# Sparse attention lane of one Trainium2 kernel, reordered by pairs of heads, with a planned moment for each part of a step

## The chip, the cores and the metric

One core of one Trainium2 chip runs the whole program. The metric is the device time of one execution in microseconds (us); lower is better. The kernel before has a median of 3911.82 us over three runs (3907.46 to 3923.37).

## What is computed

Two transformer blocks of two layers each on a sequence of 512 tokens and 1024 features, in float32. The change touches only the second block, which runs its attention stage twice, once per layer. There, six heads of 64 features in two key groups take part in three gated attentions:

```python
        s_s = jnp.einsum('bqgrd,bgqnd->bgrqn', qb, k_sel).astype(f32) * scale
        p_s = masked_softmax(s_s, key_pos <= tq[:, None])
        o_s = jnp.einsum('bgrqn,bgqnd->bqgrd', p_s.astype(v_sel.dtype), v_sel)
...
        s_w = jnp.einsum('bqgrd,bngd->bgrqn', qb, kw).astype(f32) * scale
        p_w = masked_softmax(s_w, m_w)
        o_w = jnp.einsum('bgrqn,bngd->bqgrd', p_w.astype(vw.dtype), vw)
        gt = jax.nn.sigmoid(gb.astype(f32))[..., None]
        return (gt[:, :, 0] * o_c + gt[:, :, 1] * o_s + gt[:, :, 2] * o_w).astype(qb.dtype)
```

`o_c` (not shown) goes over compressed keys, `o_s` over selected blocks, `o_w` over a window; `gt` are gates. At 512 tokens the selection and the window hold every earlier token, so that the kernel computes both as dense causal attention: the same queries against two sets of keys and values. These two are the "sparse lane". Beside it in the same stage stand the products that make the queries, keys and values of four "stick-breaking" heads, those heads themselves, the compressed attention, and a norm of each head's output.

## The kernel before, in words

The stage is `attention_region`. Each of its lanes writes a program per engine as a Python generator; a `yield` gives a planned time, and `weave` merges the lanes of an engine by these times into one fixed order of instructions. The planned times only set that order. On the chip every engine works strictly through its own list and waits at semaphores.

The lanes of the stage, by planned time in us from its start:

- the items lane (L635), 4 to 73: six products in three passes each (L493 to L495) with weights that ScalarE (L479) and VectorE (L484) split before;
- the compress lane (L2603 to L2633) and the compressed lane (L2663 to L2738), up to 76;
- the stick lane, 75 to 157: for each of four heads the scores in four blocks (L2890), masked by VectorE (L2932), then ScalarE's Abs, Exp and Ln (L2961, L2964, L2967), VectorE's L2940, running sums on TensorE (L2908) with VectorE's L2944 after each, ScalarE's Exp (L2973), the product with the values (L2920), and VectorE's copy L2950;
- the norms lane, 159 to 208: for each of eight tiles a square on ScalarE (L2999), a sum on TensorE (L3015), Ln and Exp on ScalarE (L549, L551), and a scaling on VectorE (L3022);
- the sparse lane, 2 to 198.

The sparse lane has three tiles `t` of two heads, four query blocks `qb` of 128 tokens and two kinds `m` of keys, hence 24 combinations, each for the heads `u` = 0 and 1: 48 items `n`, which it takes one after the other. The number of keys is 128, 256, 384 or 512 (`(qb + 1) * P`). An item is a score on TensorE (L2770), mask and row maximum on VectorE (L2809), the exponential with its sum on ScalarE (L2845), reciprocal, gate and scaling on VectorE (L2826, L2828, L2830), `qb + 1` transposes on TensorE (L2785), a copy out by ScalarE (L2858), and `qb + 1` products with the values on TensorE (L2796). After sixteen items VectorE adds the tile to the result (L2815), for which the norms of these tiles wait.

Head `u` = 0 lies in partitions 0 to 63 and head `u` = 1 in 64 to 127, for the queries and keys of a score as for the output of a product with values. Each step of the lane emits three parts at one planned time: on TensorE the score of item n + 2, the transposes of item n - 1, the products of item n - 2. Steps are equally long whatever their width:

```python
    def share(n):
        return (AHEAD + n) / (len(items) + 2 + AHEAD)
...
        for n in range(len(items) + 2):
            if n + 2 < len(items):
                score(n + 2)
            if 1 <= n <= len(items):
                t, qb, m, u = items[n - 1]
                pe.wait_ge(scaled, n)
```

In the trace a float32 matmul shows as two matmul records. Scores alternate between two PSUM banks (`logits[:, u]`), and a score waits until VectorE has read its bank (`shifted`).

Of the kernel before, what the change touches and what calls it, by code (L numbers as in the profile page):

```python
# [2742 lines left out]
def sparse_lane(k, r, lane, nq, ks2, kw2, vs_rows, vw_rows, cmp_out, gates, mixT, tile_out):  # L2743
# [3 lines left out]
    items = [(t, qb, m, u) for t in range(T) for qb in range(TC) for m in range(2) for u in range(2)]  # L2747
    PER_TILE = 4 * TC
# [5 lines left out]
    AHEAD = 0.6  # L2754
# [4 lines left out]
    def share(n):  # L2759
        return (AHEAD + n) / (len(items) + 2 + AHEAD)  # L2760

    @lane.tensor
    def _(pe):
        def score(n):
            t, qb, m, u = items[n]
            at, g = head(t, u)
            keys = (ks2, kw2)[m][int(g != u)]
            if n >= 2:
                pe.wait_ge(shifted, n - 1)
            nc.tensor.matmul(logits[:, u, 0:(qb + 1) * P], nq[at, t, qb * P:(qb + 1) * P], keys[at, 0:(qb + 1) * P],  # L2770
                             start=True, stop=True).then_inc(logit_done, 1)

        score(0)
        score(1)
        yield share(0)
        for n in range(len(items) + 2):
            if n + 2 < len(items):
                score(n + 2)
            if 1 <= n <= len(items):
                t, qb, m, u = items[n - 1]  # L2780
                pe.wait_ge(scaled, n)
                if n >= 3:
                    pe.wait_ge(turn_out, n - 2)
                for b in range(qb + 1):
                    last = nc.tensor.transpose(turned[:, u, b * P:(b + 1) * P], probs[:, (n - 1) % DEEP, b * P:(b + 1) * P], k.at["ident"])  # L2785
                last.then_inc(turn_done, 1)
            if n >= 2:
                t, qb, m, u = items[n - 2]
                at, g = head(t, u)
                to = out_ps[at, qb * P:(qb + 1) * P]  # L2790
                rows = (vs_rows, vw_rows)[m]
                if t and qb == m == u == 0:
                    pe.wait_ge(tile_out, t)
                pe.wait_ge(turn_out, n - 1)
                for b in range(qb + 1):
                    last = nc.tensor.matmul(to, rows[:, b, g * HD:(g + 1) * HD], probs_t[:, (n - 2) % DEEP, b * P:(b + 1) * P],  # L2796
                                            start=(m == 0 and b == 0), stop=(m == 1 and b == qb))
                last.then_inc(pv_done, 1)
            yield share(n + 1)

    @lane.vector
    def _(dve):
        def shift(n):
            t, qb, m, u = items[n]
            keys = (qb + 1) * P
            dve.wait_ge(logit_done, n + 1)
            if n >= DEEP:
                dve.wait_ge(turn_done, n - DEEP + 1)
            nc.vector.tensor_tensor_reduce(probs[:, n % DEEP, 0:keys], logits[:, u, 0:keys], k.at["causal_row"][:, S - keys:S],  # L2809
                                           -1.0, 3e38, ALU.add, ALU.min, neg_max[:, n % DEEP:n % DEEP + 1]).then_inc(shifted, 1)  # L2810

        def leave(t):
            dve.wait_ge(cmp_out, t + 1)
            dve.wait_ge(pv_done, PER_TILE * (t + 1))
            nc.vector.tensor_tensor(mixT[:, GDN_T + t, :], mixT[:, GDN_T + t, :], out_ps[:, :], ALU.add).then_inc(tile_out, 1)  # L2815

        shift(0)
        shift(1)
        yield share(0)
        for n in range(len(items)):  # L2820
            t, qb, m, u = items[n]
            p = n % DEEP
            at = probs[:, p, 0:(qb + 1) * P]
# [1097 lines left out]
```

## Time and profile before

| | us |
|---|---|
| median of three runs | 3911.82 |
| the profiled execution | 3889.2 |
| its span, first to last instruction | 3887.3 |
| TensorE matmul busy in it | 3528.6 (91%) |
| VectorE busy | 1789.5 (46%) |
| ScalarE busy | 1310.9 (34%) |
| first stage, TensorE's first to VectorE's last instruction | 2093.6 to 2314.5 |
| second stage, likewise | 3117.3 to 3338.3 |

In the rows PE is TensorE's matmul, PEld its weight load, DVE VectorE, ACT ScalarE, POOL GpSimd. A row of the timeline has start, duration from the first start to the last end, engine, line, operation, output and inputs, shapes, the number of instructions merged (x4), and in brackets the idle time before it with what ended that. The stage stands in the span twice; the rows of the two agree in their parts, and those of the first are used.

### The profile page before, as it was taken

What the parts mean: (1) busy time and instruction counts of PE and PEld (TensorE: products, weight loads), DVE (VectorE), ACT (ScalarE), POOL (GpSimd) and SP (SyncE); (2) the same over time, 40 slices, a digit from 0 to 9 for tenths busy, and PEclk for the clock granted to TensorE, in tenths of its full rate; (3) what the DMA queues carried; (4) which work ended last, traced back from release to release, by engine and by line L of the source; (5) the groups of instructions that cost most, each with busy time, mean ns of one, the idle gap of its engine ahead of it and who ended that gap; (6) DMA issues with size and microseconds to landing.
All of it is one profiled execution on the core that took longest, in us unless ns stands there. A gap on an engine that the chain in (4) does not pass through costs nothing. (4 is left out here: it accounts for less than half of the span.)

```text
span 3887.3 us, 46528 instructions
## 1 busy us (share of the span) xinstructions
PE 3528.6 (91%) x19333; PEld 2722.2 (70%) x19333; DVE 1789.5 (46%) x2765; ACT 1310.9 (34%) x2030; POOL 420.8 (11%) x351
## 2 busy tenths in 40 slices
PE   5999897999998799998998979999988899799998
PEld 4777765888686568886675647788766665477885
DVE  4775466443333433333534444444444435345534
ACT  2332453222322432322322343333343234433423
POOL 0001000220001102100122000310002300012100
PEclk7989998999999899998998999999999989899999
DMA  6651215333221112221202012232131020222230
GB/s 229 206 163 39 79 30 195 130 120 109 76 87 33 65 65 95 103 93 56 74 7 56 1 49 71 92 98 110 44 96 39 2 56 1 92 68 96 98 108 22
DMA packets 230431, 316.17 MB, mean 81 GB/s; under 512 B 13117, under 2 KB 167590, under 8 KB 228942
## 3 DMA queue, kind: packets, MB, share of 16 engines
q1 hardware_dynamic: 230222, 313.20, 24.4%
q8 instruction: 154, 2.52, 0.3%
q14 instruction: 55, 0.45, 0.0%
HBM read 310.52 MB, written 6.85 MB: 82 GB/s over the span
## 5 line engine op out<-in xcount | busy, mean ns | idle before, releaser
L493 PE MATMUL out<-h_lo,w_hi 128*128 128x512 f32 x2608 | 1042.6, 400 | 44.1 <-DVE w_lo L484 39.9
L494 PE MATMUL out<-h_hi,w_hi 128*128 128x512 f32 x2608 | 1021.7, 392 | 0.0
L495 PE MATMUL out<-h_hi,w_lo 128*128 128x512 f32 x2608 | 1021.2, 392 | 0.0
L484 DVE TENSOR_TENSOR w_lo<-ring,w_hi 128x1024 fp32r<-128x1024 f32 (+2 forms) x461 | 565.8, 1233 | 984.8 <-ACT w_hi L479 979.8
L479 ACT ACTIVATE w_hi<-ring 128x1024 fp32r<-128x1024 f32 (+2 forms) x461 | 470.9, 1027 | 1159.2 <-PE out L495 1075.1
L493 PEld LDWEIGHTS out<-h_lo,w_hi 128*128 128x128 f32 x2608 | 493.7, 189 | 168.3 <-issue 50.6
L494 PEld LDWEIGHTS out<-h_hi,w_hi 128*128 128x128 f32 x2608 | 493.6, 189 | 112.1 <-issue 11.0
L495 PEld LDWEIGHTS out<-h_hi,w_lo 128*128 128x128 f32 x2608 | 493.4, 189 | 103.8
L493 PE MATMUL item_banks<-h_lo,w_hi 128*128 128x512 f32 (+1 forms) x632 | 288.3, 456 | 14.4 <-DVE w_lo L484 5.1
L494 PE MATMUL item_banks<-h_hi,w_hi 128*128 128x512 f32 (+1 forms) x632 | 254.3, 402 | 0.0
L495 PE MATMUL item_banks<-h_hi,w_lo 128*128 128x512 f32 (+1 forms) x632 | 253.8, 402 | 0.0
L493 PEld LDWEIGHTS item_banks<-h_lo,w_hi 128*128 128x128 f32 (+1 forms) x632 | 121.6, 192 | 55.5 <-issue 22.0
L493 PE MATMUL item_banks<-w_lo,h_hi 128*128 128x256 f32 (+1 forms) x320 | 103.8, 324 | 43.4 <-DVE w_lo L484 27.3
L495 PEld LDWEIGHTS item_banks<-h_hi,w_lo 128*128 128x128 f32 (+1 forms) x632 | 121.0, 191 | 30.9
L494 PEld LDWEIGHTS item_banks<-h_hi,w_hi 128*128 128x128 f32 (+1 forms) x632 | 121.8, 193 | 28.3 <-issue 8.2
L1497 POOL TENSOR_TENSOR tiles<-temp 128x512 f32<-128x512 f32 x44 | 72.8, 1654 | 605.1 <-DVE temp L1483 324.9
L428 DVE SCALAR_TENSOR_TENSOR tiles<-tiles,c_act 128x1024 f32<-128x1024 f32 x70 | 93.8, 1340 | 57.8 <-DMA tiles<-in_mod_w 56.7
L2258 POOL TENSOR_TENSOR tiles<-tiles 128x512 f32<-128x512 f32 x64 | 76.7, 1203 | 306.4 <-ACT tiles L2244 281.9
L1629 POOL TENSOR_TENSOR xT<-xT,tiles 128x512 f32<-128x512 f32 x20 | 30.1, 1534 | 710.2 <-DVE tiles L1618 710.2
L493 PEld LDWEIGHTS item_banks<-w_lo,h_hi 128*128 128x128 f32 x320 | 64.9, 203 | 57.5 <-DVE w_lo L484 27.8
L484 DVE TENSOR_TENSOR h_lo<-tiles,h_hi 128x2048 fp32r<-128x2048 f32 (+2 forms) x43 | 83.5, 1943 | 28.4 <-ACT h_hi L479 28.4
L494 PE MATMUL item_banks<-w_hi,h_hi 128*128 128x256 f32 (+1 forms) x320 | 95.9, 300 | 0.0
(498 smaller groups left out, 4713.4 us busy)
## 6 DMA issues: line engine op xcount, KB each, us to landing
ring<-in_mlp_w SPq DMA_DIRECT2D x30, 2048.0 KB, 8.5
ring<-in_w_up SPq DMA_DIRECT2D x44, 1024.0 KB, 7.0
tiles<-in_mod_w SPq DMA_DIRECT2D x80, 512.0 KB, 4.7
ring<-in_e_w_in SPq DMA_DIRECT2D x48, 512.0 KB, 4.2
ring<-in_w_down SPq DMA_DIRECT2D x10, 2048.0 KB, 7.8
ring<-in_w_in SPq DMA_DIRECT2D x16, 1024.0 KB, 5.3
ring<-in_o_w_in SPq DMA_DIRECT2D x7, 2048.0 KB, 7.8
tiles<-in_mod_w SPq DMA_DIRECT2D x8, 1024.0 KB, 8.6
```

The lines of the kernel that those rows point to most:

```text
L428: nc.vector.scalar_tensor_tensor(total, slot, gain_of(c), total, ALU.mult, ALU.add).then_inc(summed, 1)
L479: return nc.scalar.activation(hi.bitcast(F32R), x, ACT.Copy)
L484: return nc.vector.tensor_tensor(lo.bitcast(F32R), x, hi, ALU.subtract)
L493: nc.tensor.matmul(out, wh, xl, start=start, stop=False, **kw)
L494: nc.tensor.matmul(out, wh, xh, start=False, stop=False, **kw)
L495: return nc.tensor.matmul(out, wl, xh, start=False, stop=stop, **kw)
L1497: nc.gpsimd.tensor_tensor(finish_dst(b.nth, j), acc[:, b.nth % 2, j, :], acc[:, b.nth % 2, 2 + j, :], ALU.mult).then_inc(finished, 1)
L1629: nc.gpsimd.tensor_tensor(k.xT[:, f, :], k.xT[:, f, :], temp[:, f, :], ALU.add).then_inc(pool_added, 1)
L2258: after=lambda j: nc.gpsimd.tensor_tensor(dst(j), dst(j), dst(j), ALU.mult))
```

## The change

All of it lies in `sparse_lane`. The 48 items become 24 pairs: the two heads of one (t, qb, m). Both scores of a pair follow each other directly on TensorE, behind one wait that both banks have been read. A step p has a length by its width (1.5 + qb, in units of the lane), and each part in it a planned place: scores of pair p + 1 at 0, maxima at 0.2, transposes of the two heads at 0.25 and 0.35, copies out at 0.4 and 0.6, exponentials of pair p + 1 at 0.45 and 0.65, products of pair p - 1 at 0.5 and 0.7, reciprocal, gate and scaling of pair p + 1 at 0.75, the tile's addition at 0.95. Every instruction of the lane stays; the number, the operands, the buffers and the four-deep rings are the same.

```diff
+    pairs = [(t, qb, m) for t in range(T) for qb in range(TC) for m in range(2)]
+    COST = [0.0]
+    for t, qb, m in pairs:
+        COST.append(COST[-1] + 1.5 + qb)
+    COST += [COST[-1] + 2.5, COST[-1] + 4.0]
...
-    def share(n):
-        return (AHEAD + n) / (len(items) + 2 + AHEAD)
+    def share(p, x=0.0):
+        return (COST[p] + x * (COST[p + 1] - COST[p])) / COST[-1]
...
+        def score(p):
+            t, qb, m = pairs[p]
+            if p:
+                pe.wait_ge(shifted, 2 * p)
+            for u in range(2):
...
         score(0)
-        score(1)
-        yield share(0)
...
+        for p in range(len(pairs) + 1):
+            yield share(p)
+            if p + 1 < len(pairs):
+                score(p + 1)
+            if p < len(pairs):
+                for u in range(2):
+                    n = 2 * p + u
+                    yield share(p, 0.25 + 0.1 * u)
+                    pe.wait_ge(scaled, n + 1)
...
+                    yield share(p, 0.5 + 0.2 * u)
+                    pe.wait_ge(turn_out, n + 1)
...
+        maxima(0)
+        yield share(0, 0.1)
+        normalize(0)
+        for p in range(len(pairs) + 1):
+            yield share(p, 0.2)
+            if p + 1 < len(pairs):
+                maxima(p + 1)
+                yield share(p, 0.75)
+                normalize(p + 1)
+            yield share(p, 0.95)
+            if p and p % PER_TILE == 0:
+                leave(p // PER_TILE - 1)
...
+        for p in range(len(pairs)):
+            for u in range(2):
+                n = 2 * p + u
+                yield share(p, 0.4 + 0.2 * u)
...
+                if p + 1 < len(pairs):
+                    yield share(p, 0.45 + 0.2 * u)
+                    exps(p + 1, u)
```

Three places show how the merged order moves. The first is TensorE at the start of the stage (L2770 and L2777 are scores, L2785 and L2793 transposes, L493 to L495 the items lane's first products). Before:

```order
L2770 MATMUL sparse_logits<-tiles 128x128 x2
L493 MATMUL stick_banks<-h_lo,w_hi 128x512
L494 MATMUL stick_banks<-h_hi,w_hi 128x512
L495 MATMUL stick_banks<-h_hi,w_lo 128x512
L2770 MATMUL sparse_logits<-tiles 128x128
L493 MATMUL stick_banks<-h_lo,w_hi 128x512
```

and now:

```order
L2777 MATMUL sparse_logits<-tiles 128x128 x4
L2793 MATMUL sparse_turned<-const_sb,sparse_probs 128x128 x2
L493 MATMUL stick_banks<-h_lo,w_hi 128x512
L494 MATMUL stick_banks<-h_hi,w_hi 128x512
L495 MATMUL stick_banks<-h_hi,w_lo 128x512
L493 MATMUL stick_banks<-h_lo,w_hi 128x512
```

The second pair's scores and the first pair's transposes now stand ahead of the first product of the items lane.

The second place is VectorE between the last masked score block of the first stick head (L2932, now L2946) and that head's L2940 (now L2954). Before:

```order
L2932 TENSOR_TENSOR space<-stick_banks,const_sb 128x128
L2826 RECIPROCAL sparse_sums<-sparse_sums 128x1
L2828 TENSOR_TENSOR sparse_sums<-sparse_sums,nsa_gates 128x1
L2830 TENSOR_SCALAR sparse_probs<-sparse_probs,sparse_sums 128x128
L2809 ISA sparse_probs,sparse_max<-sparse_logits,const_sb 128x256
L2809 ISA sparse_max 128x1
L2826 RECIPROCAL sparse_sums<-sparse_sums 128x1
L2828 TENSOR_TENSOR sparse_sums<-sparse_sums,nsa_gates 128x1
L2830 TENSOR_SCALAR sparse_probs<-sparse_probs,sparse_sums 128x256
L2809 ISA sparse_probs,sparse_max<-sparse_logits,const_sb 128x256
L2809 ISA sparse_max 128x1
L2940 SCALAR_TENSOR_TENSOR space<-space 128x1280
```

and now:

```order
L2946 TENSOR_TENSOR space<-stick_banks,const_sb 128x128
L2818 ISA sparse_probs,sparse_max<-sparse_logits,const_sb 128x384
L2818 ISA sparse_max 128x1
L2818 ISA sparse_probs,sparse_max<-sparse_logits,const_sb 128x384
L2818 ISA sparse_max 128x1
L2828 RECIPROCAL sparse_sums<-sparse_sums 128x1
L2830 TENSOR_TENSOR sparse_sums<-sparse_sums,nsa_gates 128x1
L2832 TENSOR_SCALAR sparse_probs<-sparse_probs,sparse_sums 128x384
L2828 RECIPROCAL sparse_sums<-sparse_sums 128x1
L2830 TENSOR_TENSOR sparse_sums<-sparse_sums,nsa_gates 128x1
L2832 TENSOR_SCALAR sparse_probs<-sparse_probs,sparse_sums 128x384
L2954 SCALAR_TENSOR_TENSOR space<-space 128x1280
```

Both scalings of one pair now stand directly ahead of the stick head's own step, and they wait for that pair's exponentials on ScalarE. There the order is, from that head's Abs (now L2975) to the second exponential of the pair:

```order
L2975 ACTIVATE space<-space 128x1280
L2978 ACTIVATE space<-space 128x1280
L2870 ACTIVATE sparse_probs_t<-sparse_turned 128x256
L2858 ACTIVATE sparse_probs,sparse_sums<-sparse_probs,sparse_max 128x384
L2870 ACTIVATE sparse_probs_t<-sparse_turned 128x256
L2981 ACTIVATE space<-space 128x1280
L2858 ACTIVATE sparse_probs,sparse_sums<-sparse_probs,sparse_max 128x384
```

The second exponential comes behind the stick head's Ln (L2981), where before one exponential of 256 columns and one copy of 128 stood between Abs and Exp, the same again between Exp and Ln, and nothing of the pair behind Ln was waited for.

The third place is ScalarE in the middle of the norms (L2999, now L3013, is a tile's square; L549 and L551 its root). Before:

```order
L2999 ACTIVATE space<-tiles 128x512
L2845 ACTIVATE sparse_probs,sparse_sums<-sparse_probs,sparse_max 128x384
L2858 ACTIVATE sparse_probs_t<-sparse_turned 128x384
L549 ACTIVATE space<-stick_banks,const_sb 128x512
L551 ACTIVATE space<-space 128x512
L2999 ACTIVATE space<-tiles 128x512
L2845 ACTIVATE sparse_probs,sparse_sums<-sparse_probs,sparse_max 128x512
L2858 ACTIVATE sparse_probs_t<-sparse_turned 128x384
L549 ACTIVATE space<-stick_banks,const_sb 128x512
L551 ACTIVATE space<-space 128x512
```

and now, at the fourth tile and after:

```order
L3013 ACTIVATE space<-tiles 128x512
L549 ACTIVATE space<-stick_banks,const_sb 128x512
L551 ACTIVATE space<-space 128x512
L2870 ACTIVATE sparse_probs_t<-sparse_turned 128x512
L3013 ACTIVATE space<-tiles 128x512
L2870 ACTIVATE sparse_probs_t<-sparse_turned 128x512
L549 ACTIVATE space<-stick_banks,const_sb 128x512
L551 ACTIVATE space<-space 128x512
L3013 ACTIVATE space<-tiles 128x512
L549 ACTIVATE space<-stick_banks,const_sb 128x512
```

From the first tile's square to the last one's, 16 activations of the sparse lane stood between those of the norms before (seven exponentials, nine copies); now it is ten (four and six), since the wider steps at the end of each tile are planned longer and the narrow ones at its start shorter.

## Rows read from the trace of the kernel before

**Rows 1.** Busy time of engines by stretch of the first stage; then granted clock, DMA.

```profile
core 0: us, PE busy (x) PEld busy (x) DVE busy (x) ACT busy (x) POOL busy (x), PEclk, DMA share, GB/s
2093.00:2113.00 20.00, 12.60 (x48) 9.03 (x48) 5.17 (x19) 4.14 (x11) 6.16 (x10) 0.60 0.82 215
2113.00:2198.00 85.00, 85.00 (x467) 60.72 (x467) 31.63 (x104) 31.68 (x71) 0.00 (x0) 0.94 0.05 13
2198.00:2279.40 81.40, 74.62 (x328) 43.16 (x328) 45.67 (x144) 39.06 (x81) 0.00 (x0) 0.96 0.00 1
2279.40:2315.00 35.60, 27.60 (x125) 14.07 (x123) 19.32 (x47) 23.45 (x48) 3.80 (x3) 0.98 0.00 0
2203.00:2212.00 9.00, 6.50 (x17) 3.50 (x18) 3.47 (x12) 4.40 (x11) 0.00 (x0) 0.62 0.00 0
```

**Rows 2.** Waits of PE in the first stage: in total, times, longest.

```profile
PE stick_banks L2908 <- DVE space L2940: 4.9, 4, 2.0
```

**Rows 3.** Timeline, start of the first stage.

```profile
2093.58 0.80 PE L2770 MATMUL sparse_logits<-tiles 64*128 64x128 f32 x4 [1.95 <-PEq L151]
...
2100.24 0.80 PE L493 MATMUL stick_banks<-h_lo,w_hi 128*128 128x512 f32 x1 [5.86 <-DVE w_lo L484]
...
2102.85 0.79 PE L2770 MATMUL sparse_logits<-tiles 64*128 64x128 f32 x2 [0.97 <-DVE sparse_max L2809]
...
2104.55 0.29 DVE L2830 TENSOR_SCALAR sparse_probs<-sparse_probs,sparse_sums 128x128 f32<-128x128 f32 x1
```

**Rows 4.** Timeline, scores on PE and what follows them directly.

```profile
2219.26 0.48 PE L2890 MATMUL stick_banks<-sb_q,sb_k 64*128 64x256 f32 x1
2219.27 0.59 PE L2770 MATMUL sparse_logits<-tiles 64*128 64x384 f32 x1
...
2245.64 0.48 PE L2770 MATMUL sparse_logits<-tiles 64*128 64x128 f32 x2
2246.06 0.66 PE L2785 MATMUL sparse_turned<-const_sb,sparse_probs 128*128 128x128 f32 x4
...
2286.55 1.12 PE L2770 MATMUL sparse_logits<-tiles 64*128 64x512 f32 x2
2287.61 0.55 PE L2785 MATMUL sparse_turned<-const_sb,sparse_probs 128*128 128x128 f32 x3
```

**Rows 5.** Timeline, from masked scores to running sums, stick heads 1, 2 and 3.

```profile
2200.49 0.62 DVE L2932 TENSOR_TENSOR space<-stick_banks,const_sb 128x256 f32<-128x256 f32 x2 [0.28 <-PE stick_banks L2890]
2201.15 1.27 ACT L2961 ACTIVATE space<-space 128x1280 f32<-128x1280 f32 x1 [2.79 <-DVE space L2932]
2206.07 1.49 DVE L2940 SCALAR_TENSOR_TENSOR space<-space 128x1280 f32<-128x1280 f32 x1 [2.04 <-ACT space L2967]
2207.62 6.21 PE L2908 MATMUL stick_banks<-space,const_sb 128*128 128x512 f32 x18 [2.00 <-DVE space L2940]
...
2219.99 0.62 DVE L2932 TENSOR_TENSOR space<-stick_banks,const_sb 128x256 f32<-128x256 f32 x2 [0.54 <-PE stick_banks L2890]
...
2226.82 2.42 PE L2908 MATMUL stick_banks<-space,const_sb 128*128 128x512 f32 x8 [1.64 <-DVE space L2940]
...
2239.10 0.62 DVE L2932 TENSOR_TENSOR space<-stick_banks,const_sb 128x256 f32<-128x256 f32 x2 [0.28 <-PE stick_banks L2890]
...
2248.29 1.99 PE L2908 MATMUL stick_banks<-space,const_sb 128*128 128x512 f32 x5 [0.56 <-DVE space L2940]
```

**Rows 6.** Timeline, the norms' sums, and the lane's widest exponential and copy.

```profile
2281.38 1.13 PE L3015 MATMUL stick_banks<-space,const_sb 128*128 128x512 f32 x2
...
2290.35 0.71 ACT L2845 ACTIVATE sparse_probs<-sparse_probs,sparse_max 128x512 f32<-128x512 f32 x1
...
2298.57 0.57 ACT L2858 ACTIVATE sparse_probs_t<-sparse_turned 128x512 f32<-128x512 f32 x1
...
2307.55 1.10 PE L3015 MATMUL stick_banks<-space,const_sb 128*128 128x512 f32 x2 [1.03 <-ACT space L2999]
...
2311.27 1.10 PE L3015 MATMUL stick_banks<-space,const_sb 128*128 128x512 f32 x2 [1.60 <-ACT space L2999]
```

More of the change, by code:

```diff
@@ L2762, in _, with width @@
+    def width(p):
+        return (pairs[p][1] + 1) * P
     @lane.tensor
     def _(pe):
[L2764 to L2771, printed above, removed]
-        score(0)
@@ L2774, in _ @@
-        score(1)
-        yield share(0)
[L2776 to L2792, printed above, removed]
-                    pe.wait_ge(tile_out, t)
[L2794 to L2799, printed above, removed]
@@ L2801, in _, with maxima @@
     @lane.vector
     def _(dve):
[L2803 to L2810, printed above, removed]
+        def maxima(p):
+            for u in range(2):
+                n = 2 * p + u
+                dve.wait_ge(logit_done, n + 1)
+                if n >= DEEP:
+                    dve.wait_ge(turn_done, n - DEEP + 1)
+                nc.vector.tensor_tensor_reduce(probs[:, n % DEEP, 0:width(p)], logits[:, u, 0:width(p)], k.at["causal_row"][:, S - width(p):S],
+                                               -1.0, 3e38, ALU.add, ALU.min, neg_max[:, n % DEEP:n % DEEP + 1]).then_inc(shifted, 1)
@@ new lines, in normalize @@
+        def normalize(p):
+            t, qb, m = pairs[p]
+            for u in range(2):
+                n = 2 * p + u
+                s, gate = n % DEEP, (1 + m) * N_NSA + 2 * t + u
+                at, total = probs[:, s, 0:width(p)], sums[:, s:s + 1]
+                dve.wait_ge(exp_done, n + 1)
+                nc.vector.reciprocal(total, total).then_inc(recip_done, 1)
+                dve.wait_ge(recip_done, n + 1)
+                nc.vector.tensor_tensor(total, total, gates[:, qb, gate:gate + 1], ALU.mult).then_inc(gated, 1)
+                dve.wait_ge(gated, n + 1)
+                nc.vector.tensor_scalar(at, at, total, None, ALU.mult).then_inc(scaled, 1)
@@ new lines, in _ @@
+        for u in range(2):
+            exps(0, u)
+        for p in range(len(pairs)):
+            for u in range(2):
+                n = 2 * p + u
+                yield share(p, 0.4 + 0.2 * u)
+                act.wait_ge(turn_done, n + 1)
+                if n >= DEEP:
+                    act.wait_ge(pv_done, n - DEEP + 1)
+                nc.scalar.activation(probs_t[:, n % DEEP, 0:width(p)], turned[:, u, 0:width(p)], ACT.Copy).then_inc(turn_out, 1)
+                if p + 1 < len(pairs):
+                    yield share(p, 0.45 + 0.2 * u)
+                    exps(p + 1, u)
```

68 lines of the change are left out of this document (26 added, 42 removed).

## The prediction

> **What bounds the kernel now.** I read the page first, and from it only that TensorE is busy for 91% of the span; since the change lies in one lane of one stage, which stands in the program twice, all that counts is which wait ends last in that stage. So I went on to the busy time by stretch [rows 1]. The stage falls into three parts. In the **first** (2093 to 2198) TensorE waits at the start, at a low clock (0.60), and is then busy for 85.0 of 85.0 us, with VectorE and ScalarE at 31 to 32: TensorE is the bound. In the **middle** (2198 to 2279.4, the stick heads) it is busy for 74.6 of 81.4 us, so something else holds it 6.8 us. The list of waits names it: 4.9 us before the running sums L2908, four times, for VectorE's L2940 [rows 2]. That is the end of a chain from the masked scores over three activations on ScalarE; the reader should see in it that whatever TensorE saves while this chain runs only lengthens its wait. In the **last** part (2279.4 to 2315, the norms) TensorE is busy for 27.6 of 35.6 us, ScalarE for 23.5; the sum L3015 waits for ScalarE's square, 1.03 us and 1.60 us in the last two of eight [rows 6].
>
> **What a pair saves on TensorE.** A score alone occupies TensorE for 0.42 us at 128 keys (2245.64 to 2246.06) and 1.06 us at 512 (2286.55 to 2287.61) [rows 4]. That is 0.21 us per 128 keys and 0.21 fixed, so 0.63 and 0.85 between. The two scores before the stage's wait stand directly behind each other already: four records take 0.80 us, where a single score's two take 0.79 at the same low clock [rows 3]. At full clock the same shows where a stick score lies next to one of the lane: they start at 2219.26 and 2219.27 [rows 4]. So I cost the second score of a pair at nothing. Its price has two ends, 0 and the full 0.42 to 1.06 us; both rows are near 0. A tile has two pairs of each width: 2 × (0.42 + 0.63 + 0.85 + 1.06) = 5.9 us, three tiles 17.8 us per stage. This is the most that scores can give, if TensorE were the bound throughout.
>
> **First part.** Before the first stick score TensorE had, by the order, six scores of 128 behind the initial two, five of 256, four each of 384 and 512: 13.3 us. One of the six belongs to the start below, 12.9 are left. It now has two pairs of 128, four of 256, two of 384 and two of 512 behind the two that stand in the wait: 7.2 us. Saved 5.7. Six more transposes and two more products have moved ahead of that point; a transpose takes 0.11 us (four 0.66, three 0.55 [rows 4]), a product, with twice the records, 0.22: +1.1. The order changes the matmul's shape (64, 128 rows, 64 columns and so on) 93 times before and 75 times now; a change costs between 0 and the 0.21 us fixed in a score [rows 4], I take 0.1. Half of the 18 lie in the scores' own cost, the rest give -0.9.
>
> Against this stands the **start**. Now the first pair's transposes stand ahead of the items lane's first product. They need both scalings, and the second of these ended at 2104.84, while the first product began at 2100.24 [rows 3]. All products queue behind the waiting transposes, so they begin near 2105.0. In those 4.8 us TensorE had waited 0.97 and done one score (0.72, counted above as gone) and some 3 us of products, at half clock: 1.5 us of work at full clock. Then the clock rises later: its return to full speed came after the unbroken run that began at 2102.85; the run now begins 2.2 us later, worth 1.1. Together +2.6 us; the ends are 1.5 (the clock rises as before) and 4.8 (everything late by the wait). First part: -5.7 + 1.1 - 0.9 + 2.6 = -2.9.
>
> **Middle part.** Here I go by the chain. After the last mask of a head it is Abs, Exp and Ln, 1.27 us each with what lies between, 3.85, then L2940, 1.49 [rows 5], in all 5.4 us bare; every activation of the sparse lane that the order puts between adds its time, 0.3 to 0.7 us (0.71 and 0.57 at 512 [rows 6], a little less in sequence, as the next starts before the last one's accumulator is read). From the end of the masks to the sums it took 6.5 us (2201.11 to 2207.62) for the first head, 6.2 for the second, 8.6 for the third [rows 5]; for the fourth about as the second.
> - First head: two scalings now stand ahead of the last mask (2 × 0.7), and behind Ln stand the second exponential of 384 (0.6) and its scaling (0.8) before L2940; between Abs and Ln one exponential and two copies replace two and two. From 9.8 us after the first score to about 13.3: **+3.5**.
> - Second head: two exponentials of 512 and two copies between Abs and Ln, 5.4 + 2.2 = 7.6 against 6.2: **+1.4**.
> - Third head: Abs, Exp and Ln now follow each other directly, 5.5 against 8.6: **-3.1**.
> - Fourth head: two exponentials and two copies, and VectorE's own backlog, some 7.5: **+0.9**.
> - Between the chains (sums to next masks), TensorE has fewer or cheaper parts: about -0.1, -1.3 and +0.3; the last two hold +1.9 each, because a pair's scalings, and once the tile's addition (L2815), now stand ahead of masks. Behind the last sums about **-1.2**.
>
> Sum +0.4 us. Its ends: the four lengthened items alone and nothing else (+6), or TensorE as the bound and all its savings real (-6: by the order and the costs above, 17.1 us of scores become 8.7, and six more transposes and products each cost 2.0).
>
> **Last part.** Seven intervals between the norms' sums take 29.9 us (2281.38 to 2311.27), 4.3 each. The last, with nothing of the sparse lane on ScalarE between, took 3.7, of which 0.5 was a wait for the last tile's addition [rows 6]: 3.2 bare. So the sparse lane's activations lengthen it: 16 before from the first square on, 10 now, as the wider steps have been given more planned time earlier. The six that leave are worth 2.9 us; besides, four of the others now fall into the 1.2 us in which ScalarE waits for a sum anyway. Walking the new order by these durations I get 26.5 us from first square to last sum against 31.9: -5.4. The ends are -2.9 and -7.4 (all intervals bare); I take -5.
>
> **Sum.** -2.9 + 0.4 - 5.0 = -7.5 us per stage, -15 for two. I take 1 off for waits that no row shows, 14 less. The profiled execution took 3889.2 us and would take 3875; the median of the runs is 22.6 us above it, so I forecast 3911.8 - 14 = **3898 us**. A measurement of this kernel can tell about 0.5%, 19.6 us, from no change.
>
> **Rivals.**
> - *TensorE is the bound everywhere.* Then the middle gives -6 instead of 0.4 and the last part -6 (three scores of 512, twelve transposes and eight products fewer): with the first part -14.9 per stage, 30 in all: 3882. For it: 92% busy in the middle, and ScalarE's waits there are mostly for TensorE's transposes, which the new places uncouple. Against: the four waits [rows 2]. The page "TensorEngine Tiling (Array Packing)" of the Trainium skill, section Key Properties, says that changing the tiling mode, other than the tile, drains the engine. By that rule the whole saving of changes counts: 195 in the stage before, 139 now, by the order; at my 0.1 us that would be 5.6 us per stage instead of the 0.9 that I count, and the rule belongs to this rival. Chance 0.25.
> - *The pair does not overlap.* If only the short scores share the array, or the two queue, scores cost what they did. Then the start's +2.6, +1.1 and -0.9 in the first part, +1.7 in the middle (nothing shorter between the chains) and -4 in the last leave +0.5 per stage: 3913. Against: both rows of overlap. Chance 0.1.
> - *Slower: the stick chain takes all the lengthening, and the clock falls.* The mechanism is VectorE's in-order list in the middle: each pair's scalings ahead of L2932 and L2940 hold the chain, +3.5, +1.4, +0.9 and 1.9 twice at the masks, 9.6 us, while the third head's gain fails because its Abs comes late too. With longer idle stretches TensorE loses its clock, as it did before the first sums: granted 0.62 from 2203 to 2212 [rows 1]; that half-speed run cost 2.1 us, at two more heads 4.3. With -2.9 in the first part and no gain in the last: +11 per stage, 3934. It decides if the waits before L2908 exceed some 14 us per stage in place of 4.9. The page "TensorE: Matmul & The Clock Gate" of the Trainium skill, Part 1, has it that idleness throttles the array to half its clock; the trace agrees with that, and the rule would make the longer waits dearer than my sum. Chance 0.08.
> - *My forecast*, chain-bound in the middle and ScalarE-bound at the end: 0.57.
>
> **How the numbers follow.** My own case runs from 3884 to 3912 by its ends, so about a tenth of its weight lies below 3892. Faster by over 0.5%: 0.25 × 0.9 + 0.57 × 0.13 = 0.3. Slower: 0.08. The rest, 0.62, within 0.5%. The range reaches down past the first rival and up past the second: 3877 to 3917.
>
> **What would show it.** Right: x4 rows of scores no longer than the x2 rows were; the first product of the items lane near 5 us later; L2908 of the first stick head some 13 us behind the first L2904 and a longer wait there, the third head's wait gone; the norms' seven intervals near 25 us; each stage about 213 us long. Wrong: a middle part several us shorter than 81 (TensorE was the bound), pairs that take the time of two, or a stage longer than 221 us.

## The result, and the profile after

The changed kernel has a median of 3872.62 us (3869.46 to 3875.04, four runs); the kernel before has 3911.89 us in the same comparison (3907.46 to 3923.37, four runs). The ratio is 0.9899, interval [0.9882, 0.9916]: 39.3 us or 1.0% faster. I had forecast 3898 us and 3877 to 3917, so the time lies below the range. Of the four executions of before, 3923.37 us lies apart from the other three. The profiled execution took 3872.61 us, its span 3870.7.

The two changed stages now last 211.1 and 210.9 us from barrier to barrier, where the profile of before has 222.2 twice: 22.4 us less together, against 15 in my sum. In the first stage, "after its start" below means after the barrier at 2092.7 us before and 2099.6 after.

Busy time by stretch of the first stage, after. The columns are those of [rows 1]. The first four answer to its first four, the last one to its fifth; the stretch of 18 us has no counterpart there.

```profile
2099.90:2119.90 20.00, 10.54 (x41) 6.76 (x41) 7.88 (x32) 5.71 (x18) 6.14 (x10) 0.60 0.84 215
2119.90:2199.60 79.70, 77.94 (x490) 59.39 (x488) 32.51 (x106) 30.47 (x71) 0.00 (x0) 0.98 0.05 14
2199.60:2280.80 81.20, 67.74 (x336) 41.60 (x336) 46.38 (x147) 39.93 (x82) 0.00 (x0) 0.94 0.00 1
2280.80:2310.70 29.90, 20.20 (x102) 10.74 (x98) 12.99 (x30) 20.32 (x38) 3.80 (x3) 0.94 0.00 0
2143.00:2161.00 18.00, 18.00 (x109) 13.48 (x109) 6.98 (x21) 4.98 (x13) 0.00 (x0) 1.00 0.11 30
2207.60:2216.00 8.40, 3.94 (x11) 2.34 (x12) 3.86 (x12) 2.16 (x6) 0.00 (x0) 0.59 0.00 0
```

The same 18 us (43.3 to 61.3 after the stage's start) in the kernel before:

```profile
2136.00:2154.00 18.00, 18.00 (x78) 12.62 (x78) 2.70 (x9) 2.36 (x6) 0.00 (x0) 0.72 0.01 3
```

What to see: up to the first stick scores the stage is 5.2 us shorter, and the last part 5.6. The middle is as long as it was (81.2 against 81.4 us [rows 1]), although TensorE is busy for 6.9 us less in it: 67.74 against 74.62. And there is a line that I had not looked for: before, TensorE was busy for 18.00 of 18.00 us at a granted clock (the share of TensorE's full clock that it was given) of 0.72, with no idle time at all, and there it is now 1.00.

Waits of PE in the first stage, after (in total, times, longest):

```profile
PE stick_banks L2922 <- DVE space L2954: 12.4, 4, 5.9
PE sparse_logits L2777 <- DVE sparse_max L2818: 9.0, 2, 8.4
PE stick_banks L3029 <- ACT space L3013: 7.3, 7, 2.1
```

The wait before the running sums, 4.9 us in [rows 2], is 12.4. TensorE's 6.9 us of saved work in the middle went into it.

Timeline of the start, after (against [rows 3]):

```profile
2109.82 0.80 PE L2777 MATMUL sparse_logits<-tiles 64*128 64x128 f32 x4 [8.45 <-DVE sparse_max L2818]
...
2110.85 1.06 PE L2793 MATMUL sparse_turned<-const_sb,sparse_probs 128*128 128x128 f32 x2 [0.23 <-DVE sparse_probs L2832]
...
2111.56 0.77 PE L493 MATMUL stick_banks<-h_lo,w_hi 128*128 128x512 f32 x1
```

The items lane's first product starts 11.9 us after the stage's start, 4.3 later than before (7.5). Both scores of a pair are one row of x4. Pairs of 384 and 512 keys at full clock, after:

```profile
2275.77 0.92 PE L2777 MATMUL sparse_logits<-tiles 64*128 64x384 f32 x4
...
2284.83 1.13 PE L2777 MATMUL sparse_logits<-tiles 64*128 64x512 f32 x4
```

Two scores of 512 take 1.13 us; one took 1.12 [rows 4]. The second score costs nothing. The page "TensorEngine Tiling (Array Packing)" of the Trainium skill, section Key Properties, states that different tiles can load weights and multiply in parallel, and the trace agrees.

Timeline from the masks of the first stick head to its sums, and the sums of heads 2 and 3, after (against [rows 5]):

```profile
2203.98 0.28 DVE L2946 TENSOR_TENSOR space<-stick_banks,const_sb 128x128 f32<-128x128 f32 x1
2204.30 1.27 ACT L2975 ACTIVATE space<-space 128x1280 f32<-128x1280 f32 x1 [2.96 <-DVE space L2946]
...
2207.90 1.26 ACT L2981 ACTIVATE space<-space 128x1280 f32<-128x1280 f32 x1
...
2209.06 0.61 ACT L2858 ACTIVATE sparse_probs<-sparse_probs,sparse_max 128x384 f32<-128x384 f32 x1
...
2210.18 0.42 DVE L2832 TENSOR_SCALAR sparse_probs<-sparse_probs,sparse_sums 128x384 f32<-128x384 f32 x1
2210.52 1.49 DVE L2954 SCALAR_TENSOR_TENSOR space<-space 128x1280 f32<-128x1280 f32 x1
...
2212.06 3.88 PE L2922 MATMUL stick_banks<-space,const_sb 128*128 128x512 f32 x8 [5.87 <-DVE space L2954]
...
2231.46 4.05 PE L2922 MATMUL stick_banks<-space,const_sb 128*128 128x512 f32 x8 [2.89 <-DVE space L2954]
...
2250.50 2.42 PE L2922 MATMUL stick_banks<-space,const_sb 128*128 128x512 f32 x8 [2.49 <-DVE space L2954]
```

Here the forecast chain can be read line by line: Ln ends at 2209.16, the pair's second exponential starts only then, its scaling at 2210.18, and the stick head's own step L2954 behind that.

The four waits are 5.9, 2.9, 2.5 and 1.1 us, each longer than before (2.0, 1.6, 0.6 and 0.7). The third is one that I had expected to see gone. Behind the second wait TensorE needs 4.05 us for the same eight records that take 2.42 at the third head: the granted clock was 0.57 there (2231.5 to 2235.5) and 1.00 at the third.

The norms' sums, after (against [rows 6]): the first, the seventh and the eighth.

```profile
2282.97 1.13 PE L3029 MATMUL stick_banks<-space,const_sb 128*128 128x512 f32 x2
...
2303.55 1.10 PE L3029 MATMUL stick_banks<-space,const_sb 128*128 128x512 f32 x2 [0.54 <-ACT space L3013]
...
2306.70 1.57 PE L3029 MATMUL stick_banks<-space,const_sb 128*128 128x512 f32 x2 [2.05 <-ACT space L3013]
```

Seven intervals take 23.7 us, 3.4 each, against 29.9 before.

So the two profiles explain 22.4 of 39.3 us by the stages. The other 17 us are not in them: all that lies outside the two stages took 3442.9 us in the profile of before and 3448.7 in that of after. The experiments had to find them.

### The profile page after: what moved, and what is told of

The parts are those of the page before. It is cut to its first block and busy times, and to the rows that moved or that the text cites. A ratio compares the mean times of both kernels' runs of the same rounds, so it can differ in the third digit from the quotient of the medians.

```text
span 3870.7 us, 46526 instructions
## 1 busy us (share of the span) xinstructions
PE 3487.1 (90%) x19333; PEld 2710.6 (70%) x19333; DVE 1783.2 (46%) x2765; ACT 1306.7 (34%) x2030; POOL 423.0 (11%) x351
## 5 line engine op out<-in xcount | busy, mean ns | idle before, releaser
L493 PE MATMUL out<-h_lo,w_hi 128*128 128x512 f32 x2608 | 1043.3, 400 | 43.6 <-DVE w_lo L484 39.3
L495 PE MATMUL out<-h_hi,w_lo 128*128 128x512 f32 x2608 | 1021.7, 392 | 0.0
L493 PEld LDWEIGHTS out<-h_lo,w_hi 128*128 128x128 f32 x2608 | 493.7, 189 | 167.4 <-issue 50.3
L495 PEld LDWEIGHTS out<-h_hi,w_lo 128*128 128x128 f32 x2608 | 493.5, 189 | 104.4
L493 PE MATMUL item_banks<-h_lo,w_hi 128*128 128x512 f32 (+1 forms) x632 | 290.4, 459 | 14.2 <-DVE w_lo L484 5.1
L495 PE MATMUL item_banks<-h_hi,w_lo 128*128 128x512 f32 (+1 forms) x632 | 254.6, 403 | 0.0
L493 PEld LDWEIGHTS item_banks<-h_lo,w_hi 128*128 128x128 f32 (+1 forms) x632 | 122.5, 194 | 55.6 <-issue 22.0
L495 PEld LDWEIGHTS item_banks<-h_hi,w_lo 128*128 128x128 f32 (+1 forms) x632 | 121.9, 193 | 31.4
L493 PE MATMUL item_banks<-w_lo,h_hi 128*128 128x256 f32 (+1 forms) x320 | 104.0, 325 | 43.8 <-DVE w_lo L484 27.7
L493 PEld LDWEIGHTS item_banks<-w_lo,h_hi 128*128 128x128 f32 x320 | 65.2, 204 | 58.0 <-DVE w_lo L484 28.2
```

The costliest lines, as they stand in the source:

```text
L493: nc.tensor.matmul(out, wh, xl, start=start, stop=False, **kw)
L495: return nc.tensor.matmul(out, wl, xh, start=False, stop=stop, **kw)
```

## The experiments

Each was timed beside the kernel before on the same chip, unless told otherwise. The ratio is to those times. "Stage" is the time between barriers of the two changed stages in the profiled execution.

### Both kernels again

No edit; each is the same code under a new name.

> The kernel before, unchanged. Its attention stage took 222.2 us twice in the profile, all other stages together 3443. The change took 11.1 and 11.3 us off the two stages, 22 in all, but 39 off the median; 17 us must lie in stages that the diff does not touch. Theory A (the other stages vary from run to run, and the profiled execution of before, 3889, was a fast one): ratio 1.000 against the kernel before, runs spread over 3889 to 3923, stages of 222.2 us, and the excess of any run over 3889 in the other stages. Theory B (something in this kernel's build makes the other stages slower whenever it is not being profiled): all timed runs near 3912, the profile near 3889 again.

> The changed kernel, unchanged. Theory A: the gain is 22 us from the two stages and the rest is spread of the other stages, so with more runs the ratio moves toward 0.994 (3889). Theory B (the change makes the other stages faster too, for instance by where it leaves the clock or the transfers): ratio again 0.990, 3872, with stages of 211 us.

Measured: the kernel before again 3910.57 us (3894.98 to 3929.6, 12 runs), ratio 1.0022 [1.0004, 1.0041]; the change again 3873.12 us (3864.11 to 3877.44, 6 runs), ratio 0.9925 [0.9900, 0.9950]; stages 222.2 and 222.2, and 211.0 and 210.9. The gain repeats, at 0.75% by the ratio where it was 1.0%. The same code against itself has an interval that leaves out 1, so ratios that differ by some 0.2% tell nothing here. What matters is how the times lie. Over all 63 executions of the kernel before in the experiments there are three heaps: 17 from 3889.6 to 3898.9 (mean clock 0.944 to 0.948), 42 from 3902.7 to 3916.4 (0.939 to 0.944) and 4 from 3927.4 to 3931.6 (0.934 to 0.937), with medians 3894.1, 3911.3 and 3929.8. Both profiles that I had so far, 3889.2 and 3894.98 us, are from the first heap; the median is from the second. (3923.37 us, from the first comparison, lies between the second and the third.) How large the gain comes out thus depends on the heaps of before: beside this run of the change, 8 of 22 were from the first. The ten executions of the change make one heap, 3864.1 to 3877.4 us.

### Only the scores paired

```diff
-            if n + 2 < len(items):
+            if n % 2 == 0 and n + 2 < len(items):
                 score(n + 2)
+                score(n + 3)
```

> Before with one edit: at every even item the two scores of a pair follow each other directly; all other places and times as before, the start too. Theory 1 (the overlap of the two scores is what gives, where TensorE is the bound): first part shorter by about 6 us per stage (13 single scores of 0.42 to 1.06 us become half as many), middle part by 0 to 2, last part by 0 to 1, stage 213 to 216 us against 222.2. Theory 2 (the planned places give, not the overlap): stage 219 to 222 us.

Measured: 3877.74 us (3872.32 to 3880.87, 6 runs), ratio 0.9938 [0.9914, 0.9962], one heap; stages 213.7 and 210.5. The first stick scores come 98.2 and 95.0 us after the stage's start instead of 105.2. In the first stage the mean granted clock up to them is 0.87 as before, so these 7.0 us are the scores and the shape changes alone; I had priced them at 5.7 and 0.9. From the first square to the last sum it takes 33.6 us (change 25.9, before 31.9). This edit of two lines gives nearly all of the change's gain, in the stages and in the heaps; the planned places shorten the last part, and their late start takes about as much.

That two stages with the same code differ by 3.2 us has a cause that shows in the clock: it rose 16 us after the start in the first and 13 in the second, and between 43 and 57 us it fell twice in the first and once in the second. The falls lie where before has its own, so pairing the scores does not remove them. The rise, one row for each stage, and the two falls of the first:

```profile
2111.80:2114.80 3.00, 3.00 (x13) 2.50 (x12) 0.00 (x0) 0.66 (x3) 0.00 (x0) 0.63 1.15 278
2141.00:2155.00 14.00, 14.00 (x57) 9.56 (x57) 2.22 (x7) 1.36 (x4) 0.00 (x0) 0.63 0.00 1
```

```profile
3128.70:3131.70 3.00, 3.00 (x23) 2.75 (x22) 0.00 (x0) 0.66 (x3) 0.00 (x0) 1.00 1.17 280
```

### The pair's scores apart again

The change, with the second score of each pair behind the first head's transposes:

```diff
-                score(p + 1)
+                score(p + 1, (0,))
...
                     last.then_inc(turn_done, 1)
+                    if u == 0 and p + 1 < len(pairs):
+                        score(p + 1, (1,))
```

> The change with one edit: the second score of a pair stands behind the first head's transposes, so that the two cannot overlap; planned places of all the rest as in the change. Theory 1 (overlap): first part longer by about 6 us per stage, middle by 1 to 3, last by 0 to 1, stage 218 to 221 us against 211. Theory 2 (planned places): stage 211 to 213 us.

Measured: 3919.95 us (3915.22 to 3926.96, 11 runs), ratio 1.0041 [1.0020, 1.0062]: slower than before, and by more than was expected, with stages of 229.0 and 239.5 us. Here the 10.5 us between two identical stages can be seen. The same 23 us of each, from 17 us after its start:

```profile
2116.70:2139.70 23.00, 23.00 (x129) 16.76 (x127) 6.77 (x28) 8.50 (x23) 0.00 (x0) 1.00 0.09 25
3150.70:3173.70 23.00, 23.00 (x71) 16.18 (x71) 4.27 (x19) 4.81 (x14) 0.00 (x0) 0.50 0.01 2
```

TensorE is busy without a gap in both, and at half clock in the second: 71 records in place of 129. The clock is not all of it: in the first stage, where it was back at 16 us too, the part up to the first stick scores is 9.2 us longer than the change's (109.2 against 100.0) and the middle 7.8 (89.0 against 81.2, at granted 0.88 against 0.94). What makes the middle so long was not taken apart. The run gave a theory for the heaps: with single scores the clock of a stage may come back some 20 to 35 us later than the 13 to 17 us that the first profiles showed.

### Pairs in the first tile only, and in the other two only

The first 16 items lie within the first 65 us or so of the stage. The edits are in the kernel before; for the first tile alone:

```diff
-            if n + 2 < len(items):
+            if n + 2 >= PER_TILE and n + 2 < len(items):
                 score(n + 2)
+            elif n % 2 == 0 and n + 2 < len(items):
+                score(n + 2)
+                score(n + 3)
```

and for the others the same with `n + 2 < PER_TILE`.

> The kernel before with the two scores of a pair together in the first of the three tiles only. Theory A (the first part gains by the scores' own time and by the clock, which fell to half for 10 to 13 us in the first tile's time of the stages of before without any idle time of TensorE, and in the executions of before near 3910 it falls for longer): half-clock stretches between 40 and 62 us after the stage's start shorter than before's, stage 215 to 217 us, and the runs in one group: median 3875 to 3882. Theory B (before's two groups of runs, 3890 and 3910, have another cause elsewhere in the program): the stage's gain of 5 to 7 us shows all the same, but the runs split in two groups 20 us apart, most of them in the upper one: median 3895 to 3900.

> The kernel before with the two scores of a pair together in the second and third tile only. Theory A: the first 60 us of the stages as before, with the half-clock stretches of before; stage about 219 to 221; the runs in two groups as before's: median 3903 to 3908. Theory B: the same, since the cause is elsewhere. Rival C (the gain lies in the later tiles): stage 214 to 216, median 3880 to 3885.

Measured: first tile 3882.97 us (3880.28 to 3892.27, 6 runs, five of them within 2.8 us; the sixth, 9 us above them, I can't explain), ratio 0.9932 [0.9910, 0.9955]; stages 215.8 and 215.8. Later tiles 3901.92 us (3893.66 to 3928.29, 12 runs; the kernel before beside them 3911.21, 17 runs), ratio 1.0000 [0.9978, 1.0021]: the medians are 9 us apart and the ratio sees no difference, because both spread over their heaps. Its profile fell on the slowest execution: 3928.29 us, both stages 240.2. The same 34 us of both stages, first with pairs in the first tile (from 16.6 us after the start), then without (the same place):

```profile
2113.50:2147.50 34.00, 34.00 (x202) 26.60 (x201) 10.24 (x38) 12.21 (x26) 0.00 (x0) 0.95 0.14 36
3130.60:3164.60 34.00, 34.00 (x203) 26.60 (x202) 10.24 (x38) 12.21 (x26) 0.00 (x0) 0.95 0.14 35
```

```profile
2110.50:2144.50 34.00, 34.00 (x109) 26.52 (x108) 4.44 (x18) 8.11 (x16) 0.00 (x0) 0.50 0.08 20
3154.90:3188.90 34.00, 34.00 (x109) 26.52 (x108) 4.44 (x18) 8.11 (x16) 0.00 (x0) 0.50 0.08 20
```

Up to there the two kernels differ in nothing but whether the two scores of a pair stand together. Without that, the clock stayed at its lower level from the barrier to 50 us after it, in this execution; the same order in the first profile of before had it back at 16 and 13 us. With the pairs together, the first stick scores come at 99.2 us, 6.0 earlier than before, against the 5.5 that my price gives for the first tile's seven pairs behind the first (5.9 less 0.42). Theory A holds for the first tile, though not by the falls between 40 and 62 us: there the profile has 10.2 us at the lower level, as in the first stage of before. What went is the late clock. For the later tiles it was off: I had expected stages of 219 to 221 us, a median of 3903 to 3908 and heaps as before's. The profiled execution has a late clock in both stages, the median is 3902, and the executions lie in other heaps (seven from 3894 to 3902, three near 3914, two above 3920). I don't explain these. With the first tile paired, pairs in the other two as well shorten the first stage from 215.8 us to only 213.7.

### The kernel before once more

One profiled execution; no edit.

> The kernel before once more, for a profile of one execution. Theory A: if it comes out near 3890, both changed stages are 222.2 us long and TensorE's clock is at full from 14 to 17 us after their start; if near 3910, one of the two stages is 18 to 20 us longer, because the clock stays at half until 40 to 51 us after its start, and if near 3929, both are. Theory B: a slow execution has both stages at 222.2 us and its 20 us in other stages.

Measured: 3910.68 us, the heap in which the median lies. Its first stage lasts 239.0 us, its second 222.2; all that lies outside them took 3447.6. Both stages whole, and the 34 us from 16.6 us after the start of each:

```profile
2097.40:2336.40 239.00, 216.95 (x962) 139.53 (x962) 102.06 (x314) 98.39 (x208) 9.93 (x13) 0.85 0.09 23
3138.10:3360.30 222.20, 200.41 (x962) 126.86 (x962) 101.49 (x314) 98.27 (x208) 10.01 (x13) 0.92 0.10 25
```

```profile
2114.00:2148.00 34.00, 34.00 (x110) 26.52 (x109) 4.43 (x18) 8.11 (x15) 0.00 (x0) 0.50 0.08 20
3154.70:3188.70 34.00, 34.00 (x171) 24.29 (x170) 10.33 (x38) 12.30 (x26) 0.00 (x0) 0.90 0.14 35
```

The same 962 matmul records take 216.95 us of TensorE in one stage and 200.41 in the other. 16.8 us is the distance between the stages, and the heaps' medians lie 17.2 and 18.5 apart: none, one or both stages with a late clock. (That each execution of the second heap has exactly one, and each of the third two, is inferred from time and mean clock; this one shows one.) The excess of an execution of before thus lies in the changed stages, and neither theory of the first two runs had that.

Counted over all profiles: where the scores of the first tile stand singly (five profiles, ten stages), the clock was still at its lower level 40 us after the stage's start in four; where they stand in pairs (nine profiles, 18 stages), it had risen by 16.5 us in every one.

### Equal steps

```diff
-        COST.append(COST[-1] + 1.5 + qb)
+        COST.append(COST[-1] + 3.0)
```

> The change with all steps equally long (3.0 units each, as the 1.5 to 4.5 of the change are on the mean). Theory (weighting the steps by width is what shortens the norms): from the first tile's square to the last norm sum it takes 32 to 34 us again instead of 25.9, and each changed stage about 216 us instead of 211; median about 3884. Rival (pairs alone are worth it, the weighting nothing): last part 26 to 28 us, stages 211 +- 1, median 3873.

Measured: 3878.33 us (3873.19 to 3881.76, 5 runs), ratio 0.9916 [0.9895, 0.9938]; stages 209.5 and 213.2. Neither number of the theory came: from first square to last sum 28.6 us, not 32 to 34, and the first stick scores 4.4 us earlier than the change's, since fewer of the lane's parts stand ahead of them and, for 1.7 us in the first stage, since the clock doesn't fall there (1.00 from 16.5 us after the start up to them). The weights move work between the parts of the stage, and equal steps in place of the change's cost little, 3878 against 3873 us. The last part, 33.6 us with paired scores alone, is shorter mainly because of the planned places (28.6), and less because wide steps are planned longer (25.9). Between the squares stand 16, 14 and ten of the lane's activations, so 5.0 us go with two of them and 2.7 with four: their number isn't the price.

### The items lane's first product ahead again

```diff
-    COST = [0.0]
+    COST = [1.0]
```

> The change with the lane's steps one unit (2.5 us) later, so that the items lane's first product stands ahead of the second pair's scores and the first pair's transposes again. Theory (the start costs what TensorE waits there): the first product begins 7.6 us after the stage's start instead of 11.9, the first stick scores come 2 to 4 us earlier than 100.0, stage 207 to 209, median 3866 to 3869. Rival 1 (hidden: the first part is then held by VectorE and ScalarE): stage 211, median 3873. Rival 2 (the clock rises later or falls again because the run of products is broken by a wait): first part longer by 2 to 5 us, median 3875 to 3883.

Measured: 3878.11 us (3872.32 to 3885.14, 5 runs), ratio 0.9917 [0.9895, 0.9939]; stages 214.0 and 212.0. The first product does start at 7.5 us, 4.3 earlier, but the first stick scores come at 101.1 and 97.8, on the mean 0.6 earlier than the change's 100.0. The clock of rival 2 is there, at the place where the kernel before fell too, 43.4 to 61.4 us after the start:

```profile
2137.00:2155.00 18.00, 17.40 (x84) 13.60 (x84) 5.14 (x18) 2.90 (x7) 0.00 (x0) 0.72 0.11 30
```

Its first part is not 2 to 5 us longer, though: what makes the stages longer than the change's is mostly the middle, 83.1 us in the first stage against 81.2. The run gives the price of the late start: up to the first stick scores the mean granted clock is 0.87 here and 0.90 in the change, 3.3 us of full-clock work, and yet they come only 1.1 us later. The late start costs the rest, 2.2 us.

### Half the weight, scalings apart, and both

```diff
-        COST.append(COST[-1] + 1.5 + qb)
+        COST.append(COST[-1] + 2.25 + 0.5 * qb)
```

```diff
-                yield share(p, 0.75)
-                normalize(p + 1)
+                yield share(p, 0.6)
+                normalize(p + 1, (0,))
+                yield share(p, 0.8)
+                normalize(p + 1, (1,))
```

> The change with steps of 2.25 + 0.5 x query block, halfway between the change's 1.5 + 1 x and the equal 3.0. With equal steps the first stick scores came 4.4 us earlier, the middle took 0.5 to 4 us longer and the last part 2.7. Theory (the weights move work between parts that have different limits, and in the middle and last part TensorE waits for a chain): first scores at 97 to 98, last part 26 to 27.5, stage 207 to 210, median 3866 to 3872. Rival (what one part gains the next one loses, and what is left is where the clock falls): stage 211 to 213, median 3873 to 3878.

> The change with the two heads' scalings of a pair at 0.6 and 0.8 of the step in place of both at 0.75. Theory (VectorE waits in its list for the pair's second exponential, and the stick head's step and the running sums wait behind that: 5.9 us at the first head, 2.9 at the second): the waits before the running sums shrink by 2 to 5 us in a stage; stage 207 to 210, median 3866 to 3870. Rival (ScalarE's Abs, Exp and Ln set the wait, whatever VectorE does): waits and stage as in the change, 211 us, median 3873.

> Both edits together, half the weight and the scalings at 0.6 and 0.8. Theory: the two gains add, stage 204 to 208, median 3860 to 3868, and it is faster than the change by more than 0.1%. Rival: no better than the change, 3873 +- 4, since the clock's falls take back what the waits give.

Measured: half the weight 3862.06 us (3856.12 to 3864.13, 5 runs), ratio 0.9878 [0.9851, 0.9905], stages 206.7 and 205.4; scalings apart 3875.82 us (3869.36 to 3878.47, 6 runs), ratio 0.9913 [0.9887, 0.9938], stages 212.3 and 212.0; both 3860.17 us (3856.78 to 3864.03, 5 runs), ratio 0.9875 [0.9844, 0.9905], stages 205.2 and 205.2. Waits before the running sums in the first stage, half weight:

```profile
PE stick_banks L2922 <- DVE space L2954: 2.9, 4, 1.0
```

and with the scalings apart:

```profile
PE stick_banks L2924 <- DVE space L2956: 12.4, 4, 5.2
```

Scalings apart do nothing: the four waits add up to 12.4 us as in the change, so what holds the chain is not that VectorE takes both scalings in one place. The half weight puts the lane's parts at other places beside the four stick heads, and the waits fall to 2.9 us. The stage gains less, 4.4 us, and more than was expected all the same (206.7 and 205.4, not 207 to 210). With both edits the two gains do not add: 3860 is the half weight alone, since the scalings give nothing. The two versions with half the weight are faster than both kernels: 3862 and 3860 us against the change's 3873, timed at another hour and on another chip beside the same kernel before, whose median was the same (3909.24 and 3909.08); their slowest runs (3864.13 and 3864.03) are level with the fastest of the change's ten (3864.11), while the intervals of the ratios just touch.

## Why the prediction was wrong

Most mechanisms of the stage were right; two numbers were not, and one of them, the distance from a profiled execution to the median, I had not taken for a part of the change at all.

- **A pair's second score is free: right.** 1.13 us for two of 512 against 1.12 for one. The first tile alone gave 6.0 us where its price says 5.5.
- **First part, -2.9: it was -5.2.** The runs give the terms for the first stage. Scores and shape changes: -7.0, from the pairs alone at the same clock (forecast -6.6). More of the lane's parts ahead of the first stick scores: +2.9, from the run with the first product ahead against the one with paired scores alone, 101.1 against 98.2 at the same 0.87 (forecast +1.1). The late start: +2.2 (forecast +2.6, with 1.1 for a later rise of the clock; in this stage it rose 16.2 us after the start before and 16.3 after, in the second 13.0 and 16.3). And one term that I had at nothing: at the same place the granted clock was 0.72 over 18 us before and is 1.00 now, which is 5.0 us of full-clock work; the change has one fall of its own instead, later and shorter (0.66 over 5 us, 1.7). That is 3.3 gained. By the runs it belongs to the planned places, not to the pairing: with paired scores alone the falls stay, and one unit later in the planned places they are back. I had read the first part as "85.0 of 85.0 us busy" and not asked why its mean clock was 0.94 [rows 1]. The failed term is that I counted the clock only where TensorE had waited. The fall that the change still has:

```profile
2170.00:2175.00 5.00, 4.93 (x28) 4.36 (x29) 2.82 (x12) 0.59 (x1) 0.00 (x0) 0.66 0.01 3
```

- **Middle, +0.4: it was -0.3.** Sums of the first head 12.4 us after its first score (forecast 13.3, before 9.8); from masks to sums 7.4, 5.5 and 6.6 us for heads 2 to 4 (forecast 7.6, 5.5 and 7.5). The savings of TensorE went into the wait before the sums, 4.9 to 12.4 us. One of the signs that I had named failed: the third head's wait is not gone but 2.5 us (before 0.6), because its masks end later, and from its first score to its sums it takes 10.9 us against 11.8, a gain of 0.9 and not 3.1. Of the slower rival its clock came in part: one more head, the second, ran its sums at a fallen clock. The rest is refuted: 12.4 is under the 14 from which it would decide, and the third head's chain did shorten. So is TensorE as the bound everywhere, although its time, 3882, was nearer.
- **Last part, -5.0: it was -5.6**, from first square to last sum 25.9 us (forecast 26.5). The reason I gave, that activations of wide steps leave this part, covers less than half: equal steps, with four more of these activations, lost only 2.7 us of it.
- **The sum, -14, was -22.4**: 2.3 us more in the first part of each stage, 0.7 in the middle and 0.6 in the last, and the 1 us that I took off for waits.
- **"The median of the runs is 22.6 us above it": the step that failed.** I carried the distance between before's profiled execution and its median over to the changed kernel, as if it were a constant. It was 16.8 us of late clock in one of the two stages, which the profiled execution happened not to have, and 5.8 us outside them (3442.9, the shortest such part of all profiles, against 3448.7 in the second profile of before and in that of the change). The late clock goes with the pairs: none of the change's ten executions has it by its time, and neither of its two profiles. The 5.8 us stay, and the sum comes out: 3889.2 - 22.4 + 5.8 = 3872.6. As two whole executions: before, usual, 3447.6 + 222.2 + 239.0 = 3908.8 us of span, and the changed one 3448.7 + 211.1 + 210.9 = 3870.7, a difference of 38.1 where 39.3 was measured between the medians.

The warning was there: the three times shown, 3907 to 3923, all lay 18 us or more above the profiled 3889, where the change's own four lie within 5.6 us of each other.

## What to carry to other kernels

Where two matmuls of 64 rows work on different halves of the partitions, let them stand directly behind each other in TensorE's list; two lines in the loop gave 6 us here in the first tile, where TensorE is busy almost all the time, and 2 in the other two together, where the waits for other engines lie. If the profiled execution is faster than every timed one, the profile doesn't show the execution that the median measures: look at the mean clock of both, and take a second profile, before adding a difference to the median. A stretch that is busy without a gap can still run at half clock; read the granted clock by stretch as well as the waits.

## What the runs showed of the hardware

TensorE's clock stayed at 1.2 GHz (granted 0.50) through 34.00 us without an idle moment in the records, in which it worked through 110 records with the scores single; where they stood in pairs the same stretch had 202 records at 0.95. Which of two identical stages it met changed from one execution to the next: none in two profiles of the kernel before and the first in the third; the second and both were seen in kernels that also have single scores in the first tile. It also fell in the middle of unbroken work (0.72 over 18.00 busy us). The page "TensorE: Matmul & The Clock Gate" of the Trainium skill, Part 1, has it that the clock comes back at a point that varies between runs, and calls the cost of coming back under 1% of a typical kernel. The trace agrees that the point varies, here between 13 and 50 us after the stage's start, and the 16.8 us between an early and a late return are 0.4% of 3909. For a change of 1%, that was nearly half of what was measured. The same page says that sustained activity brings the clock back. The rows with single scores differ from that, 34 us without a gap and no return, and here the measurement decides. Why single scores keep the clock low, their changes of shape or their own short work, was not tried apart.
